# A two-layer encoder trunk on one core: the first weight block and the first input tiles in three pieces, and VectorE's weight splits placed behind the scaling of the probabilities

## The reference, cut to what matters

```python
def hybrid_layer(x, ...):
    h = rms_norm(x, norm_w)
    proj = jnp.einsum('bld,dn->bln', h, w_in)        # 272 tokens x 2048 -> 5824 columns
    (aq, ak, av, ag, bq, bk, bv, bg, cq, ckv, ckr, cg, du, dg) = jnp.split(proj, split_points, axis=-1)
    ya = diff_attention(aq, ak, av, ...)             # 4 heads, two softmax maps each
    yb = axial_gqa(bq, bk, bv, ...)                  # 4 query heads, 2 key/value heads
    yc = latent_attention(cq, ckv, ckr, ...)         # low-rank latents, 4 heads
    yd = multiscale_pool(du, ...)
    y = jnp.concatenate([ya * silu(ag), yb * silu(bg), yc * silu(cg), yd * silu(dg)], axis=-1)
    return x + jnp.einsum('bln,nd->bld', y, w_out)   # 2048 x 2048
```

## Time and profile before

| | |
|---|---|
| runs, us | 904.98, 906.03, 904.94 (median 904.98) |
| profiled execution, us | 905.02 |
| its span, first to last instruction, us | 903.2 |
| mean granted clock of TensorE | 0.999 |
| PE busy | 895.9 us, 99% |
| DVE busy | 639.5 us, 71% |
| ACT busy | 566.5 us, 63% |
| SP's transfers | 142.64 MB, 44.4% of the 16 DMA engines' time |

### The profile page before, as it was taken

The page is one execution under the profiler, slowest core; times in us unless marked ns, Lnnn a source line. Parts: engine busy times, 40 slices in busy tenths (PEclk is TensorE's granted clock), DMA queues, the critical chain, the costliest instruction groups (busy, mean ns, idle before and its releaser), DMA issues.

```text
span 903.2 us, 18071 instructions
## 1 busy us (share of the span) xinstructions
PE 895.9 (99%) x7070; PEld 860.0 (95%) x7070; DVE 639.5 (71%) x1074; ACT 566.5 (63%) x986; POOL 0.2 (0%) x4
## 2 busy tenths in 40 slices
PE   8999999999999999999999999999999999999998
PEld 7999998998999999999999999999999999999998
DVE  7785887778777776766665659887687667766552
ACT  7678756577666667745454588556686666665331
POOL 0000000000000000000000000000000000000000
PEclk9999999999999999999999999999999999999999
DMA  8754333343434443445455544334435344445561
GB/s 333 264 197 140 134 140 137 124 136 115 145 139 143 139 149 130 147 147 190 172 199 186 188 176 151 118 120 176 149 97 184 140 141 157 152 158 187 187 217 64
DMA packets 22996, 143.83 MB, mean 159 GB/s; under 512 B 2560, under 2 KB 4736, under 8 KB 6528
## 3 DMA queue, kind: packets, MB, share of 16 engines
q1 hardware_dynamic: 22768, 142.64, 44.4%
q10 hardware_dynamic: 144, 0.04, 0.1%
HBM read 140.58 MB, written 2.10 MB: 158 GB/s over the span
## 4 chain that ended last, share of the span: by engine, by line
PE 97%; ACT 1%; DMA 1%; SPq 0%; DVE 0%; issue 0%; ACTq 0%; DVEq 0%
PE dense L736 27%; PE dense L738 26%; PE dense L737 26%; PE s_ps L907 4%; PE o_ps L943 4%; PE norm_ps L862 2%; PE t_ps L922 2%; DMA raw<-w_stream_dram 1%; ACT w_hi L1039 1%; PE swap_ps L738 0%; PE norm_ps L738 0%; PE norm_ps L737 0%; PE swap_ps L737 0%; PE swap_ps L736 0%; PE norm_ps L736 0%; PE norm_ps L951 0%
## 5 line engine op out<-in xcount | busy, mean ns | idle before, releaser
L736 PE MATMUL dense<-h_hi,w_hi 128*128 128x272 f32 (+2 forms) x1440 | 427.1, 297 | 2.3 <-DVE h_lo L1328 2.3
L738 PE MATMUL dense<-h_hi,w_lo 128*128 128x272 f32 (+2 forms) x1440 | 412.7, 287 | 0.0
L737 PE MATMUL dense<-h_lo,w_hi 128*128 128x272 f32 (+2 forms) x1440 | 410.9, 285 | 0.0
L1348 DVE TENSOR_TENSOR w_lo<-raw,w_hi 128x1024 fp32r<-128x1024 f32 (+1 forms) x256 | 312.0, 1219 | 86.5 <-ACT w_hi L1039 80.3
L1039 ACT ACTIVATE w_hi<-raw 128x1024 fp32r<-128x1024 f32 (+1 forms) x256 | 270.3, 1056 | 70.4 <-PE dense L738 56.1
L736 PEld LDWEIGHTS dense<-h_hi,w_hi 128*128 128x128 f32 x1440 | 271.3, 188 | 7.9 <-issue 2.8
L737 PEld LDWEIGHTS dense<-h_lo,w_hi 128*128 128x128 f32 x1440 | 271.4, 188 | 1.2
L738 PEld LDWEIGHTS dense<-h_hi,w_lo 128*128 128x128 f32 x1440 | 271.1, 188 | 0.0
L736 PE MATMUL dense<-y_hi,w_hi 128*128 128x272 f32 (+1 forms) x500 | 143.6, 287 | 0.2
L738 PE MATMUL dense<-y_hi,w_lo 128*128 128x272 f32 (+1 forms) x500 | 142.7, 285 | 0.0
L737 PE MATMUL dense<-y_lo,w_hi 128*128 128x272 f32 (+1 forms) x500 | 142.4, 285 | 0.0
(11 more groups left out here) (175 smaller groups left out, 808.1 us busy)
## 6 DMA issues: line engine op xcount, KB each, us to landing
raw<-w_stream_dram SPq DMA_DIRECT2D x128, 1024.0 KB, 4.8
out_dram<-x SPq DMA_DIRECT2D x8, 256.0 KB, 4.7
x<-xt_dram SPq DMA_DIRECT2D x3, 544.0 KB, 8.9
raw<-w_stream_dram SPq DMA_DIRECT2D x3, 512.0 KB, 7.6
con<-consts_dram SPq DMA_DIRECT2D x1, 984.0 KB, 7.8
x<-xt_dram SPq DMA_DIRECT2D x2, 272.0 KB, 4.8
raw<-w_stream_dram SPq DMA_DIRECT2D x2, 256.0 KB, 4.6
d_w<-consts_dram SPq DMA_DIRECT2D x2, 256.0 KB, 5.3
```

The source lines that it names most:

```text
L736: nc.tensor.matmul(ps, whi, xhi, start=first, stop=False)
L737: nc.tensor.matmul(ps, whi, xlo, start=False, stop=False)
L738: return nc.tensor.matmul(ps, wlo, xhi, start=False, stop=last)
L1348: signal(nc.vector.tensor_tensor(w_lo[:, g % RING, 0:n], raw[:, e % RAW, CHUNK * half:CHUNK * half + n], w_hi[:, g % RING, 0:n].bitcast(F3 ...
```

## The change

Three things change. (1) Chunk 0.0 and input tiles 0 to 3 come in three pieces: a quarter of the chunk with tile 0, a quarter with tile 1, half with tiles 2 and 3. The weight pieces are issued by SP, the input pieces by ScalarE ahead of its table load, with the load of `par` second among them. (2) In the plans of ScalarE and VectorE, tiles 4 and 5 are split ahead of chunk 0.2 (at -6.5) instead of behind it. (3) VectorE's splits of the chunks of slots 27 to 94 in both layers stand at 1 + 0.491 + 0.03 instead of 0.71 behind their slot, right behind the `s_scale` of the next slot.

```diff
+FIRST = [(0, 1), (1, 2), (2, 4)]
...
+LATE_SPLITS = (27, 95)
...
         if kind in at_engine:
-            plan.append((slot + at_engine[kind] + MOVED.get(stage, 0), len(plan), stage))
-
-    for n in (0, 1):
-        plan += [(-11, 2 * n, ("split_half", n)), (-11, 2 * n + 1, ("x_half", n))]
+            place = at_engine[kind] + MOVED.get(stage, 0)
+            if kind == "split" and at_engine is AT_VECTOR and LATE_SPLITS[0] <= stage[2] < LATE_SPLITS[1]:
+                place = 1 + at_engine["s_scale"] + 0.03
+            plan.append((slot + place, len(plan), stage))
+
+    for n in range(len(FIRST)):
+        plan += [(-11, 2 * n, ("split_part", n)), (-11, 2 * n + 1, ("x_part", n))]
...
-    plan += [(-5, 0, ("x_first", 0, 1)), (-3, 0, ("x_first", 0, 2)), (2.9, 0, ("x_first", 0, 3))]
+    plan += [(-6.5, 0, ("x_first", 4, 6)), (-5, 0, ("x_first", 6, 8)), (-3, 0, ("x_first", 8, 12)),
+             (2.9, 0, ("x_first", 12, 16))]
...
-        for n in (0, 1):
-            at = slice(CHUNK // 2 * n, CHUNK // 2 * n + CHUNK // 2)
-            sp.dma_start(raw[:, 0, at], w_stream[0, :, at]).then_inc(s_first[0] if n else s_half, 16)
-            sp.dma_start(x[:, 2 * n:2 * n + 2, :], xt[:, 2 * n:2 * n + 2, :]).then_inc(s_x[0] if n else s_x_half, 16)
+        for n, (a, b) in enumerate(FIRST):
+            at = slice(256 * a, 256 * b)
+            sp.dma_start(raw[:, 0, at], w_stream[0, :, at]).then_inc((*s_part, s_first[0])[n], 16)
...
         def setup(_):
+            act.dma_start(x[:, 0:1, :], xt[:, 0:1, :]).then_inc(s_x_part[0], 16)
             act.dma_start(par[:, :], params).then_inc(s_par, 16)
+            act.dma_start(x[:, 1:2, :], xt[:, 1:2, :]).then_inc(s_x_part[1], 16)
+            act.dma_start(x[:, 2:4, :], xt[:, 2:4, :]).then_inc(s_x[0], 16)
```

More of the change, by code:

```diff
@@ L792, in first_chunk @@
             for k in range(CK):
-                if k == 0:
-                    pe.wait_ge(half_lo, 1)
-                if k == CK // 2:
+                if k < 2:
+                    pe.wait_ge(part_lo, k + 1)
+                if k == 2:
                     pe.wait_ge(lo_ready, 1)
@@ L976, in setup, with split_part @@
         def setup(_):
+            act.dma_start(x[:, 0:1, :], xt[:, 0:1, :]).then_inc(s_x_part[0], 16)
             act.dma_start(par[:, :], params).then_inc(s_par, 16)
+            act.dma_start(x[:, 1:2, :], xt[:, 1:2, :]).then_inc(s_x_part[1], 16)
+            act.dma_start(x[:, 2:4, :], xt[:, 2:4, :]).then_inc(s_x[0], 16)
             nc.scalar.preload_act_table_set("natural_log_exp_and_others")
[L980 to L983, removed]
+        def split_part(n):
+            at = slice(256 * FIRST[n][0], 256 * FIRST[n][1])
+            act.wait_ge((*s_part, s_first[0])[n], 16)
+            signal(nc.scalar.activation(w_hi[:, 0, at], raw[:, 0, at], ACT.Copy), part_hi if n < 2 else hi_ready,
+                   (1, 2, 1)[n])
         def second_half(n):
@@ L989, in second_half, with x_part, x_first @@
             signal(nc.scalar.activation(w_hi[:, 1, at], raw[:, 0, of], ACT.Copy), (second_hi, hi_ready)[n], 1 + n)
-        def x_half(n):
+        def x_part(n):
             if n == 0:
                 act.wait_ge(s_par, 16)
-            act.wait_ge((s_x_half, s_x[0])[n], 16)
-            for kt in (2 * n, 2 * n + 1):
+            act.wait_ge((*s_x_part, s_x[0])[n], 16)
+            for kt in range(*FIRST[n]):
                 x_hi(0, kt)
-        def x_first(_, c):
-            act.wait_ge(s_x[c], 16)
-            for kt in range(4 * c, 4 * c + 4):
+        def x_first(a, b):
+            act.wait_ge(s_x[a // 4], 16)
+            for kt in range(a, b):
                 x_hi(0, kt)
@@ L1222, in p_out @@
             signal(nc.scalar.activation(p_t[0:32, 4, at_q:at_q + nq], turned_tails(b, nq), ACT.Copy), pt_ready, k + 1)
-        run = dict(setup=setup, split_half=split_half, second_half=second_half, x_half=x_half, lift=lift, x_first=x_first, x_square=x_square, lam_exp=lambda_exp,
+        run = dict(setup=setup, split_part=split_part, second_half=second_half, x_part=x_part, lift=lift, x_first=x_first, x_square=x_square, lam_exp=lambda_exp,
                    x_out=x_out, split=split,
@@ L1258, in setup, with split_part @@
             nc.vector.memset(odd_only[0:16, :], 0.0).then_inc(tails_zero, 1)
-        def split_half(n):
-            at = slice(CHUNK // 2 * n, CHUNK // 2 * n + CHUNK // 2)
-            dve.wait_ge((half_hi, hi_ready)[n], 1)
+        def split_part(n):
+            at = slice(256 * FIRST[n][0], 256 * FIRST[n][1])
+            dve.wait_ge(part_hi if n < 2 else hi_ready, (1, 2, 1)[n])
             signal(nc.vector.tensor_tensor(w_lo[:, 0, at], raw[:, 0, at], w_hi[:, 0, at].bitcast(F32), ALU.subtract),
-                   (half_lo, lo_ready)[n], 1)
+                   part_lo if n < 2 else lo_ready, (1, 2, 1)[n])
         def second_half(n):
@@ L1270, in second_half, with x_part, x_first @@
                    (second_lo, lo_ready)[n], 1 + n)
-        def x_half(n):
+        def x_part(n):
             if n == 0:
                 dve.wait_ge(s_par, 16)
-            dve.wait_ge((s_x_half, s_x[0])[n], 16)
-            for kt in (2 * n, 2 * n + 1):
+            dve.wait_ge((*s_x_part, s_x[0])[n], 16)
+            for kt in range(*FIRST[n]):
                 x_lo(0, kt)
-        def x_first(_, c):
-            dve.wait_ge(s_x[c], 16)
-            for kt in range(4 * c, 4 * c + 4):
+        def x_first(a, b):
+            dve.wait_ge(s_x[a // 4], 16)
+            for kt in range(a, b):
                 x_lo(0, kt)
@@ L1526, in s_scale @@
             signal(last, w_ready, k + 1)
-        run = dict(setup=setup, split_half=split_half, second_half=second_half, x_half=x_half, x_first=x_first, x_add=x_add, lam_dot=lam_dot, lam_out=lam_out,
+        run = dict(setup=setup, split_part=split_part, second_half=second_half, x_part=x_part, x_first=x_first, x_add=x_add, lam_dot=lam_dot, lam_out=lam_out,
                    x_out=x_out, split=split, rescale=rescale, sq_sum=sq_sum, rope_mid=rope_mid, rope_turn=rope_turn, rope_fin=rope_fin,
```

4 lines of the change are left out of this document (2 added, 2 removed).

## The result

The changed kernel takes 910.72 us (median of 6 runs, 908.65 to 911.86) against 905.05 (904.94 to 906.03, 6 runs): ratio 1.006, 95% interval 1.0047 to 1.0073. It is slower by 5.7 us where 1.6 was forecast, and outside the range. The profiled execution took 911.64 (span 909.9), 6.6 us above the one before.

What follows compares the result with a forecast made beforehand. TensorE, 97% of the chain, was taken to bound the kernel. Start -0.85, late splits +2.65 and earlier scaling -0.1 gave +1.7 us on 905.02, or 906.7, stated as 906.6 us; range 903.9 to 907.8.

Steps and rivals of the forecast that it cites:

- the part on pieces and issuing engine: At the start: smaller first pieces and ScalarE's issuing are worth nothing by themselves; one more split costs ScalarE about 0.2 us.
- nothing is to be had from it: TensorE's clock: granted at 1.00, the 2.4 GHz level, in both stretches shown, so no gain there.
- The order of tiles: At chunk 0.2: splitting tiles 4 and 5 earlier lets TensorE start at 13.75 to 14.0 and run faster, -0.85 us.
- the prediction's own test: At the start: if TensorE takes up chunk 0.2 at 14.25 or later, the first part of the sum is wrong.
- its first term: The start of the kernel, up to TensorE's work on chunk 0.2: -0.85 us, bounds 0 and -1.1.
- The late splits: TensorE waits for w_lo at chunks 1.79 (1.45 us), 1.71 (0.35) and 0.61 (0.85): +2.65; earlier scaling gives -0.1.
- The small gain: Earlier scaling shortens TensorE's 0.3 us wait for copied probabilities: -0.1 us, between 0 and -0.4.
- The start gives nothing: Rival, chance 0.14: small pieces and second queue cancel the earlier tiles' gain, late splits cost as forecast, 907.6 us.

Runs made afterwards that it cites:

- s_only: The changed kernel with VectorE's late splits back at their old places, so only the changed start remains: 908.06 us.
- s_by_sync: s_only, but SyncE instead of ScalarE issues the input pieces, in turn with the weight pieces: 906.65 us.
- w2x2: s_by_sync with weights and input of the first chunk both loaded in halves, still split in three steps: 904.72 us.
- w2x3: s_by_sync with the weights of the first chunk loaded in halves, the input still in three pieces: 905.92 us.
- w3x2: s_by_sync with the input loaded in two halves, the weights still in three pieces: 906.28 us.
- both runs with three and three: s_by_sync and its repeat, weights and input each in three pieces, all issued by SyncE: 906.65 and 906.76 us.
- fill: s_only plus three matmuls on zeros in front of the second and third k-step of chunk 0.0: 906.41 us.
- tiles_only: The kernel before with one edit, input tiles 4 and 5 split ahead of chunk 0.2: 904.11 us.
- l_but_59: l_only with chunks 0.59, 1.71 and 1.79 left at their old places: 905.37 us.
- l_only: The kernel before with only VectorE's late splits added: 907.56 us.
- two tiny loads: tiles_only plus two loads of 64 bytes a partition that nobody reads, issued by SyncE or by ScalarE: 904.73 and 904.64 us.
- hold_sync: s_only, but SyncE issues nothing after its three weight pieces until the last input piece has landed: 908.33 us.

## Why the prediction was wrong

- **Where the time goes.** Against 905.1: the order of tiles -1.0; the first chunk in three steps +0.6; small transfers +2.0; ScalarE as the issuer +1.4 (`s_only` against `s_by_sync`), through the clock; late splits +2.4. Sum 5.4 of the 5.7 measured; the rest is within the spread of the changed kernel's start. These are differences along one order of steps, and in another order the middle ones would come out otherwise: 0.28 us of the +0.6 is the wait at 402 us, which the changed kernel does not have, so that at the start ScalarE as the issuer stands for about 1.7.
- **The step that failed** is in the part on pieces and issuing engine: "An earlier first matmul only makes TensorE wait longer for chunk 0.2, because that chunk's landing does not move: the same bytes stand ahead of it. Worth nothing by itself". It took the path through the landing of chunk 0.2, and that landing as fixed. Both are wrong. In the changed kernel the path leads through input tiles 2 and 3, landed at 10.25 where the second input half was there at 7.19 before: TensorE stops twice inside chunk 0.0 and goes on at 11.63, which makes 1.4 of the 3.97 us, and its clock falls, which makes 2.5. And the landing moves: I counted bytes and took the rate of the earlier trace rows for them, but the rate from 4 to 7 us fell from 382 to 253 GB/s in the changed kernel, and to about 200 with all six small pieces on one queue. There, in `s_by_sync`, it is chunk 0.2 that TensorE waits for, at 15.79. Shown by `w2x2`, `w2x3`, `w3x2` and both runs with three and three.
- **What I didn't look at** belongs to the same step. I looked at when the first piece and chunk 0.2 come, and not at the pieces between them. With two queues the loads did not land in the order in which one queue had delivered them, so tiles 1 to 3 came late. That a second issuer adds no bandwidth, the rule that I cited, wasn't the question.
- **The clock.** The prediction said of it that "nothing is to be had from it". That is true, but something was to be lost. No rival had it. It explains part of the scatter of the changed kernel, 3.2 us where the kernel before keeps within 1.1: its three executions at a mean clock of 0.996 took 911.16 to 911.86, the one at 0.998 took 910.08, and the two at 1.000 took 908.65 and 910.29. `fill` shows the clock's part.
- **The order of tiles** was right: -0.85 forecast, -1.0 measured, with chunk 0.2 at 13.66 against 13.75 to 14.0. The forecast had the third step of splitting in it, which `tiles_only` has not; with it, in `w2x2`, chunk 0.2 starts at 13.96 and chunk 0.3 0.73 us earlier than before. In the changed kernel itself nothing of it could be seen; by the prediction's own test (chunk 0.2 at 14.25 or later, there 18.70) its first term was wrong as a whole.
- **The late splits** were right: +2.65 and -0.1 forecast, +2.39 measured, at the three places named, 0.95, 0.35 and 1.45 us where 0.85, 0.35 and 1.45 were forecast. The mechanism at 0.61, the gap before the scaling, is confirmed by `l_but_59`. The small gain was right by luck: it was to come from the wait of 0.3 us for copied probabilities, which is still there in `l_only`, 0.3 us, once; 0.2 us came at 1.33 instead.
- **The rivals.** "The start gives nothing" (907.6) named the small pieces and the second queue, but allowed them only to cancel the gain. A start that loses had no rival: I had bounded that term at 0, which is why the range ended at 907.8.
- **Open:** why a packet takes longer among small pieces; why the wait at 402 us comes with some starts and not with others; what the rest of the 0.6 us of the three-step split and of the 0.5 us of two tiny loads is made of; which of TensorE's halts lower its clock.

## What to carry to other kernels

Cut a first load smaller only after having looked at what the transfer rate does in the trace, for the first matmul gains less than the chunks behind it lose: here 1.4 us of earlier start (`s_by_sync` began at 5.79 instead of 7.15) went with a third chunk that came 1.5 later. Before TensorE begins earlier, look whether the operands of its next matmuls are there: in the changed kernel a halt of 2.0 us was followed by 2.5 us lost to the clock, and `fill` avoided that by giving TensorE something to do. On a second queue look at every small load, the parameters too. Where an operation is moved out of a stretch in which its engine waits, look for what will fill that stretch: the price is the gap, and it comes out somewhere else than at the moved operation.

## What the runs showed of the hardware

- Loads on ScalarE's and SyncE's queues got equal numbers of packets (238 and 243 from 4 to 7 us), which gives bytes in proportion to the packets' size (0.21 and 0.55 MB), and the landings of the two queues alternated, load by load, from 5.1 to 10.2 us.
- Cutting 256 and 272 KB loads into 128 and 136 KB ones lowered the rate of all DMA engines together from 384 to about 200 GB/s for 3 us (`w2x2` against both runs with three and three).
- In the changed kernel TensorE stood still from 7.6 to 9.7 us; at 10.3, after five more matmuls, its clock fell to the 1.2 GHz level and stayed there until 17.2: 2.5 us lost on 24 matmuls. In `s_only` a halt of 1.30 us up to 9.09 was followed by the same, the clock at 0.50 from 10 to 14. In `hold_sync` halts of 1.86 and 1.48 us were not (1.000 in 4 executions of 4). Three matmuls on zeros in the halts prevented it in 11 executions of 11, where 4 of 6 had it without them.
